# High and low activations of 66 up projection slabs in one matmul of 512 columns, their sum on VectorE

## The reference, cut to what matters

```
def conv_ffn(h, w_up, conv_w, conv_b, w_down, valid):      # first network
    up = h @ w_up                                            # 1024 -> 2 x 2816
    a, b = split(up)
    acc = conv_b + sum(a_pad[:, j:j + L] * conv_w[j] for j in range(3))
    return (silu(acc) * b) @ w_down

def swiglu(x, w_gate, w_up, w_down):                        # second network
    return (silu(x @ w_gate) * (x @ w_up)) @ w_down

def second_block(...):
    for l in range(2):
        h = h + 0.5 * swiglu(rmsnorm(h), ffn1 weights of l)
        h = h + hybrid_mixer_2(rmsnorm(h), ...)
        h = h + 0.5 * swiglu(rmsnorm(h), ffn2 weights of l)
    return rmsnorm(h)[:, 16:]
```

## Time and profile before

| | us |
|---|---|
| median of 3 runs | 1461.64 (1461.39 to 1462.56) |
| the profiled execution, its own time | 1462.14 |
| its span, first to last instruction | 1460.3 |
| TensorE busy | 1452.9 (99%) |
| VectorE busy | 903.3 (62%) |
| ScalarE busy | 767.8 (53%) |
| GpSimd busy | 493.8 (34%) |

### The profile page before, as it was taken

One profiled execution on the slowest core, in us unless ns is written; L12 is line 12 of the kernel. 1 busy time (PEld: TensorE's weight loads), 2 busy tenths in 40 slices (PEclk: granted clock), 3 DMA queues, 4 the chain that ended last, 5 costly groups with the idle time before them and its releaser, 6 DMA issues.

```text
span 1460.3 us, 30910 instructions
## 1 busy us (share of the span) xinstructions
PE 1452.9 (99%) x11465; PEld 1421.6 (97%) x11465; DVE 903.3 (62%) x1576; ACT 767.8 (53%) x1097; POOL 493.8 (34%) x212
## 2 busy tenths in 40 slices
PE   9999999999999999999999999999999999999998
PEld 8999999889999999999999999999999999999987
DVE  6438888756445469988644434444447898864533
ACT  6556565555444446567544544444444657654443
POOL 6551000533334303710333442433420570044342
PEclk9999999999999999999999999999999999999999
DMA  7435566645556445445555654555644545567663
GB/s 262 137 102 160 176 196 192 213 157 172 173 172 212 163 130 165 141 156 162 175 176 172 207 180 129 183 173 183 199 151 145 173 118 186 174 193 202 208 189 114
DMA packets 74635, 250.92 MB, mean 172 GB/s; under 512 B 15809, under 2 KB 16705, under 8 KB 74561
## 3 DMA queue, kind: packets, MB, share of 16 engines
q1 hardware_dynamic: 74272, 249.38, 54.6%
q10 hardware_dynamic: 288, 0.54, 0.1%
HBM read 247.79 MB, written 1.05 MB: 170 GB/s over the span
## 4 chain that ended last, share of the span: by engine, by line
PE 98%; DVE 1%; ACT 0%; issue 0%; DVEq 0%; ACTq 0%
PE W L1685 27%; PE W L1686 27%; PE W L1687 27%; PE W L1773 3%; PE XP L1837 3%; PE XQ L1837 2%; PE W L1772 1%; PE W L1737 1%; PE W L1788 1%; PE W L1787 1%; PE W L1738 1%; PE W L1786 1%; PE W L1739 1%; PE XQ L1949 0%; PE XP L1842 0%
## 5 line engine op out<-in xcount | busy, mean ns | idle before, releaser
L462 POOL TENSOR_TENSOR wlo<-raw,whi 128x1024 fp32r<-128x1024 f32 (+1 forms) x185 | 473.2, 2562 | 915.4 <-ACT whi L536 914.9
L1685 PE MATMUL W<-xh,whi 128*128 128x272 f32 (+2 forms) x2400 | 689.8, 287 | 0.0
L1686 PE MATMUL W<-xl,whi 128*128 128x272 f32 (+2 forms) x2400 | 687.0, 286 | 0.0
L1687 PE MATMUL W<-xh,wlo 128*128 128x272 f32 (+2 forms) x2400 | 685.9, 286 | 0.0
L536 ACT ACTIVATE whi<-raw 128x1024 fp32r<-128x1024 f32 (+1 forms) x440 | 480.9, 1098 | 128.9 <-PE W L1687 89.6
L1685 PEld LDWEIGHTS W<-xh,whi 128*128 128x128 f32 x2400 | 452.3, 188 | 2.2 <-issue 1.2
L1687 PEld LDWEIGHTS W<-xh,wlo 128*128 128x128 f32 x2400 | 452.1, 188 | 0.0
L1686 PEld LDWEIGHTS W<-xl,whi 128*128 128x128 f32 x2400 | 451.3, 188 | 0.2
L1011 DVE TENSOR_TENSOR wlo<-raw,whi 128x1024 fp32r<-128x1024 f32 (+1 forms) x255 | 331.7, 1302 | 80.5 <-ACT whi L536 80.1
L1685 PE MATMUL W<-ax,whi 128*128 128x272 f32 (+2 forms) x816 | 234.4, 287 | 0.4 <-DVE ax L1455 0.3
L1686 PE MATMUL W<-ax,whi 128*128 128x272 f32 (+2 forms) x816 | 234.4, 287 | 0.0
(11 more groups left out here) (288 smaller groups left out, 1405.1 us busy)
## 6 DMA issues: line engine op xcount, KB each, us to landing
raw<-in_w SPq DMA_DIRECT2D x377, 512.0 KB, 3.7
raw<-in_w SPq DMA_DIRECT2D x64, 704.0 KB, 4.1
proj<-proj SPq DMA_DIRECT2D x16, 64.0 KB, 3.6
scr<-in_cst SPq DMA_DIRECT2D x1, 1000.0 KB, 8.6
h<-in_hT SPq DMA_DIRECT2D x3, 272.0 KB, 5.2
raw<-in_w SPq DMA_DIRECT2D x2, 256.0 KB, 4.1
proj<-in_gain SPq DMA_DIRECT2D x1, 512.0 KB, 4.6
out<-proj SPq DMA_DIRECT2D x4, 128.0 KB, 1.8
```

The source lines that it names most:

```text
L462: pool.tensor_tensor(wlo[:, j, 0:cols], raw[:, j, 0:cols], whi[:, j, 0:cols].bitcast(F32), ALU.subtract).then_inc(lo_ready[j], 1)
L1685: pe.matmul(out, whi[:, j, w], mh, start=start and k == 0, stop=False, skip_group_check=True)
L1686: pe.matmul(out, whi[:, j, w], ml, start=False, stop=False, skip_group_check=True)
L1687: ins = pe.matmul(out, wlo[:, j, w], mh, start=False, stop=stop and k == len(rhs) - 1, skip_group_check=True)
```

## The change

`xh` and `xl` become the two halves of one tile `xx`, chunk by chunk. In the 22 up slabs (slots 1 and 3) of the first network's up projection, and in all 44 slabs of the last layer's second one, TensorE issues two matmuls for each chunk instead of three: wlo by xh on 256 columns, then whi by xh and xl on 512 columns. The bank then holds two halves. VectorE adds them with a `tensor_reduce` over pairs, read from PSUM into SBUF, waits for that result on the semaphore `half_added`, and multiplies the sum by `rinv`. The gate slabs of the first network, which have 258 columns, stay as they are. `tail_logits` writes 32 output rows for each of its four products instead of 128, and `tail_values` splits each product in two, of 64 rows and 16 columns.

```diff
-        xh = sb("xh", [P, DC, T], F32R)
-        xl = sb("xl", [P, DC, T], F32R)
+        xx = sb("xx", [P, DC, 2, T], F32R)
+        xh, xl = xx[:, :, 0, :], xx[:, :, 1, :]
...
-            return prod[:, b, t:] if conv else W[2 * b + 1][:, t:T]
+            return prod[:, b, t:] if conv else W[2 * b + 1][:, 0:T - t]
...
+            def scaled_halves(out, total, bank, n, added):
+
+                dve.wait_ge(mm_done, n)
+                dve.tensor_reduce(total, W[bank][:, :].rearrange("p (s n) -> p n s", s=2), mybir.AxisListType.X, ALU.add).then_inc(half_added, 1)
+                dve.wait_ge(half_added, added)
+                return dve.tensor_tensor(out, total, rinv[:, T_B:], ALU.mult)
...
-                        if j % 2 == 0:
+                        if j % 2 == 0 and ta == T_B:
+                            scaled_halves(gate[:, b, 2 + T_B:T + 2], gate[:, b, 2 + T_B:T + 2], j, n, added + 4 * i + j + 1).then_inc(evac_done, 1)
+                        elif j % 2 == 0:
                             scaled(gate[:, b, 2 + ta:T + 2], j, n, ta).then_inc(evac_done, 1)
...
-                            up = upv[:, tb:] if conv else W[j][:, tb:T]
-                            scaled(up, j, n, tb).then_inc(evac_done, 1)
+                            up = upv[:, tb:] if conv else W[j][:, 0:T - tb]
+                            if tb == T_B:
+                                scaled_halves(up, upv[:, T_B:], j, n, added + (2 * i + b + 1 if conv else 4 * i + j + 1)).then_inc(evac_done, 1)
+                            else:
+                                scaled(up, j, n, tb).then_inc(evac_done, 1)
...
+            def in_halves(j, k):
+
+                w = slice(k * P, k * P + P)
+                both = W[j][:, :].rearrange("p (s n) -> p s n", s=2)
+                pe.matmul(W[j][:, 0:T - T_B], wlo[:, j, w], xh[:, k, T_B:], start=k == 0, stop=False, skip_group_check=True)
+                return pe.matmul(both, whi[:, j, w], xx[:, k, :, T_B:], start=False, stop=k == DC - 1, skip_group_check=True)
+
+            def project_halves(g, j):
+
+                emptied(4 * g + j - 3)
+                pe.wait_ge(lo_ready[j], g + 1)
+                for k in range(DC):
+                    ins = in_halves(j, k)
+                ins.then_inc(mm_done, 1)
...
-                    ins = mm(out, qz[:, c, :], proj[:, FK + 2 * c, :], False)
+                    rows = slice(32 * c, 32 * c + 32)
+                    ins = mm(out[rows, :], qz[:, c, rows], proj[:, FK + 2 * c, :], False)
...
-                    ins = mm(X[3][:, FOX_W + w * c:FOX_W + w * c + w], vT[:, b, P * c:P * c + P],
-                             probT[:, 0, P * b + w * c:P * b + w * c + w], b == 0)
+                    for half in range(2):
+                        p0, q0, q1 = 64 * half, w * c + w // 2 * half, w * c + w // 2 * (half + 1)
+                        ins = mm(X[3][p0:p0 + 64, FOX_W + q0:FOX_W + q1], vT[:, b, P * c + p0:P * c + p0 + 64],
+                                 probT[:, 0, P * b + q0:P * b + q1], b == 0)
```

More of the change, by code:

```diff
@@ L1053, in residual_halves @@
                                          ALU.mult, ALU.add).then_inc(half_added, 1)
-                dve.wait_ge(half_added, DC * r + m + 1)
+                dve.wait_ge(half_added, FC + DC * r + m + 1)
                 dve.scalar_tensor_tensor(h[:, bass.ds(m, 1), T_B:], W[bank][:, T - T_B:], coef, h[:, bass.ds(m, 1), T_B:],
@@ L1072, in ffn_up @@
                 early = 2 if own[1] else 1
+                added = 0 if conv else FC + DC
                 def group(i, own, nxt, first=False):
@@ L1720, in project, with first_pair @@
                 slab(g, j, rhs, W[j][:, t:T], each=each, between=between).then_inc(mm_done, 1)
+            def in_halves(j, k):
[9 more added lines that the diff above has]
+                ins.then_inc(mm_done, 1)
             STAT_AT = 5
-            def first_pair(g, rhss, each, behind=(3, 3), t=(0, 0), norm=None):
+            def first_pair(g, rhss, each, behind=(3, 3), t=(0, 0), norm=None, joined=(False, False)):
                 for j in range(2):
@@ L1734, in first_pair @@
                     for j in range(2):
[L1735 to L1739, removed]
+                        if joined[j]:
+                            ins = in_halves(j, k)
+                        else:
+                            mh, ml = rhss[j][k]
+                            out = W[j][:, t[j]:T]
+                            pe.matmul(out, whi[:, j, w], mh, start=k == 0, stop=False, skip_group_check=True)
+                            pe.matmul(out, whi[:, j, w], ml, start=False, stop=False, skip_group_check=True)
+                            ins = pe.matmul(out, wlo[:, j, w], mh, start=False, stop=k == DC - 1, skip_group_check=True)
                         if k == DC - 1:
@@ L1748, in ffn_up @@
                     pe.wait_ge(meta_sum, 1)
-                first_pair(g, (x_rhs(ta), x_rhs(tb)), (xl_ready, split_base(p)), t=(ta, tb), norm=p)
+                joined = (ta == T_B, tb == T_B)
+                first_pair(g, (x_rhs(ta), x_rhs(tb)), (xl_ready, split_base(p)), t=(ta, tb), norm=p, joined=joined)
                 if fin:
@@ L1754, in ffn_up @@
                     t = tb if j % 2 else ta
-                    project(g, j, x_rhs(t), t=t)
+                    if joined[j % 2]:
+                        project_halves(g, j)
+                    else:
+                        project(g, j, x_rhs(t), t=t)
                 with pe.Fori(1, N_UP) as i:
@@ L1760, in ffn_up @@
                             pe.wait_ge(al_ready, FC * f + 2 * i - 1 + j // 2)
-                        project(g + i, j, x_rhs(t), t=t)
+                        if joined[j % 2]:
+                            project_halves(g + i, j)
+                        else:
+                            project(g + i, j, x_rhs(t), t=t)
             def halves(g, j, f, half, out, first):
```

## The result

The changed kernel takes 1482.91 us (median of 4 runs, 1482.76 to 1483.25) against 1461.55 us, a ratio of 1.0145 with a 95% interval of 1.0127 to 1.0163. It is 21.4 us slower, where no difference was predicted. The granted TensorE clock is 1.00 here and 0.999 before, so the clock plays no part.

A forecast was written before the change was run, and what follows sets the result against it. TensorE was taken as the bound, with 98% of the chain. From the profiled 1462.14 us: - 2.6 (joins) - 0.3 (attention) + 1.3 + 1.5 (standstills) = 1462.0, or 1461.5 us as median, no difference; range 1458.3 to 1466.5.

The forecast's parts named there:

- The step that failed: Scaling behind the new reduce, both stages: moving its input from PSUM to SBUF was to leave its price unchanged.
- The room in the last layer: Last layer's second up projection, after the start: VectorE, half busy per 5.68 us slab pair, fits two reduces of 1.46 us.
- Rival (b): A pair costs double, so VectorE sets the first network's pace, lap 12.20 us against 11.28: 1473.5 us in all; chance 0.18.
- TensorE's gain: Joined slabs of both up projections: 528 chunks each 5.0 ns cheaper, 2.6 us, 0.9 in the first network, 1.7 last layer.
- Standstills at the start: TensorE waits for late VectorE in each stage's first slabs: 1.3 us in the first network, 1.5 us in the last layer.
- The laps in the first network: First network's up projection: VectorE's lap over four slabs grows from 10.67 to 11.14 us, still under TensorE's 11.28.
- The attention edits: Attention: tail_logits gains 1.2 us, tail_values costs 0.9 in four places; together 0.3 us gained.

The follow-up runs named there:

- the last layer alone: The changed kernel with the first network's up projection as before; attention edits and the last layer's 44 joined slabs stay: 1481.53 us, ratio 1.0133.
- the layout alone: The kernel before with one edit, xh and xl as halves of one tile, chunk by chunk; no matmul or VectorE instruction added or removed: 1462.06 us, ratio 1.0002.
- the sum in the other bank: The changed kernel with all halves summed into a free PSUM bank, so the scaling reads one input from PSUM: 1460.13 us, ratio 0.9990.
- GpSimd's work made short: The changed kernel, but GpSimd makes only 128 of 1024 columns of each low weight slab in the last layer's second up projection: 1458.94 us, one run.

## Why the prediction was wrong, point by point

**The step that failed.** "The scaling itself goes from a PSUM to an SBUF input; it stays at its price." It has two inputs, and the other one was in SBUF already. With both there it waits for GpSimd: 2014 ns in the mean of 22, where the kernel's other scalings take 425: 35 us more of VectorE's time in one stage. The runs with the sum or the norm factor in PSUM, at 1460.13 and 1460.82 us, show that this is the whole loss. The Trainium skill states it (SBUF — State Buffer, Who interferes with whom): "A DVE instruction with two SBUF inputs contends with a GpSimd instruction that reads SBUF". The traces agree: the scaling ends 0.29 us after GpSimd's instruction. The prediction weighed a section on TensorE and not this one, which bears on the very instruction whose input the change moves.

**The room in the last layer.** "it has room for the 1.46 us of two reduces" was right as far as it went: VectorE at 73.33 of 95 us with two reduces per pair, and TensorE not waiting. With the long scalings the lap of four slabs is 1408.63 - 1395.58 = 13.05 us:

```profile
1395.58 2.40 DVE L1034 TENSOR_TENSOR W<-scr,rinv 128x256 f32<-128x256 f32 x1
...
1408.63 2.40 DVE L1034 TENSOR_TENSOR W<-scr,rinv 128x256 f32<-128x256 f32 x1
```

TensorE needs 11.2 (32 chunks of 350 ns). The nine laps from 1289.70 to 1408.63 us take 13.2 in the mean, 2.0 more than TensorE needs: 18.1 us. Against the 123.40 us of the stage without a wait, its 144.52 us are 21.1 longer; the other 3.0 are standstills ahead of 1289.70. VectorE then enters the last down projection late, and that takes 2.3 us more than before, 1.5 of them by the view in one wait on line 1824. The last 1.1 of the 3.5 us behind the up projection lie after the last output copy has been issued. They are not the scalings': the run with the norm factor in PSUM has them too, and the run with the last layer alone, with its long scalings, has not. What they are is open.

**Rival (b)** had the right form, VectorE setting the pace, but the wrong place and cause: a pair costs nothing extra (682 ns), and in the loop of the first network, where GpSimd is idle, VectorE's lap of 11.16 us stays under TensorE's of 11.4 (16 joined chunks of 350.5 ns and 16 gate chunks of 363.0).

**TensorE's gain.** 1.7 us in the last layer: 123.40 against 125.21 us where nothing waits, 1.8. In the first network 0.9 was expected; against the layout alone it is 1.2 with two slabs fewer joined, but the layout takes 1.6 back. The distances between starts show it as well: joined chunks stand 350.5 ns apart in the first network (160 to 250 us), and 350.0 in the last layer with the sum in the other bank (1300 to 1385 us).

**Standstills at the start.** First network 1.3 predicted, and none behind it. TensorE at the slab that waits for the `wlo` of slot 2, and the matmul ahead of it:

```profile
151.74 0.40 PE L1740 MATMUL W<-xx,whi 128*128 128x512 f32 x1
153.16 0.35 PE L1698 MATMUL W<-xx,whi 128*128 128x258 f32 x1 [1.03 <-DVE wlo L1011]
```

Joined matmuls of 512 columns stand 0.23 us ahead of the next elsewhere, here 1.42: 1.2 us. Last layer 1.5 predicted; with the sum in the other bank the stage lasts 124.92 us against 123.40 where nothing waits, 1.5. The size was right and the reason was not whole: the prediction put the late first scaling down to the norm factor. In the kernel before that is done at 1276.92 us, and the scaling starts at 1279.57 because the `wlo` between them takes 2.58 us beside GpSimd instead of 1.21. Where this `wlo` is short, in the run with GpSimd's work made short, the stage has no standstill.

The laps in the first network: 10.67 us became 11.14 by forecast. VectorE's two rows of the changed kernel, one lap apart:

```profile
166.53 0.49 DVE L1101 SCALAR_TENSOR_TENSOR scr<-scr,prm 128x256 f32<-128x256 f32 x1 [0.15 <-DVE scr L1098]
...
177.69 0.48 DVE L1101 SCALAR_TENSOR_TENSOR scr<-scr,prm 128x256 f32<-128x256 f32 x1 [0.15 <-DVE scr L1098]
```

11.16 us. Reading the rows wait by wait gave this term rightly.

**The attention edits.** 0.3 us predicted, 1.2 measured. `tail_logits` gained 1.23, as forecast. The mis-sized term is `tail_values`, which was to cost 0.9: its 12 records of 64 rows and 16 columns take 0.46 us, 38 ns each, and not the 67.5 of the records with 128 columns, so those were the wrong ones to take the price from. It costs nothing. It gains nothing either: each of the four places is 0.12 us shorter, but the attention edits are 1.0 us ahead right behind `tail_logits` (70.59 us against 71.59) and still 1.0 ahead where the up projection starts.

**What the forecast left out** is the layout: TensorE's distances were taken to be independent of where the operands lie. Its three terms, + 1.6, - 2.0 and + 0.6, happen to cancel, so it did not move the total.

## What to carry to other kernels

When an edit moves an operand of a VectorE instruction, list for that instruction where both inputs lie, and look in GpSimd's timeline for what runs beside it. One input in PSUM keeps it free of GpSimd; two in SBUF can make a 0.43 us instruction last until GpSimd is done, and the other engines' waits may lock the two together so that it happens every time. A stage that VectorE enters late has no room at its start, whatever its mean load: leave the first group as it was.

## What the runs showed of the hardware that was not expected

The distance between matmuls changes with where the moving operand lies. With `xh` and `xl` chunk by chunk in one tile (2176 bytes a chunk) instead of two tiles (1088 bytes a chunk each), and nothing else changed, the sum of three distances goes from 378.3 to 376.6 ns for 272 columns (330 to 440 us), from 355.0 to 356.7 for 256 (1300 to 1385 us), and from 351.6 to 356.6 for 256 and 359.2 to 363.4 for 258 in the first network (160 to 250 us); all are means of over 120 chunks. In the kernel before, the three matmuls of a chunk of 256 columns stand 116.3, 119.7 and 119.0 ns apart from 1300 us on and 117.9, 116.5 and 117.2 from 160 us on, for the same instructions. Which property of the address does this was not tried, and stays open. It is worth up to 1.6 us a stage here, as much as the change was to gain.
